# Two changes in one trunk kernel: softmax reciprocals spread by transfers, and the start of the up projection reordered

## The reference

```python
proj = (rmsnorm(x, norm1_g) * (1 + sc1) + sh1) @ w_in
y = concatenate([ssd_mixer(p_ssd), mla_mixer(p_mla), swa_sink_mixer(p_swa)]) @ w_out
x = x + g1 * y
h = rmsnorm(x, norm2_g) * (1 + sc2) + sh2
u = causal_dwconv(h @ ffn_w_up, ffn_conv_w, ffn_conv_b)      # width 3
a, b = split(u, 2)                                           # 2816 columns each
x = x + g2 * ((silu(a) * b) @ ffn_w_down)
```

## Time and profile before

| | |
|---|---|
| median of 3 runs | 2294.43 us (2293.14 to 2296.67) |
| the profiled execution's own time | 2295.75 us |
| its span | 2294.0 us |
| mean granted TensorE clock | 0.991 |
| attention, layer 0 | 326 to 431 us |
| start of the up projection, layer 0 | 541 to 606 us |

### The profile page before, as it was taken

One profiled execution on the slowest core, in us unless ns is written; L12 is line 12 of the kernel. 1 busy time (PEld: TensorE's weight loads), 2 busy tenths in 40 slices (PEclk: granted clock), 3 DMA queues, 4 the chain that ended last, 5 costly groups with the idle time before them and its releaser, 6 DMA issues.

```text
span 2294.0 us, 31143 instructions
## 1 busy us (share of the span) xinstructions
PE 2250.7 (98%) x11377; PEld 1844.6 (80%) x11377; DVE 1642.4 (72%) x2280; ACT 1104.0 (48%) x1818; POOL 974.6 (42%) x634
## 2 busy tenths in 40 slices
PE   6999999999999999999999999999999999999998
PEld 6887868887788888888878787788878888888887
DVE  7985466458878887778898744762796666667886
ACT  5355557444444444444543464772444444444455
POOL 3222322445988888300002124153399777760000
PEclk7999999999999999999999999999999999999999
DMA  9742220341444443577457222224323333337763
GB/s 331 283 136 69 66 74 20 129 143 43 160 127 140 118 142 106 170 280 252 146 211 249 63 70 62 50 86 132 105 83 97 115 93 117 94 124 272 255 203 115
DMA packets 273606, 317.13 MB, mean 138 GB/s; under 512 B 33869, under 2 KB 188288, under 8 KB 272687
## 3 DMA queue, kind: packets, MB, share of 16 engines
q1 hardware_dynamic: 271663, 312.11, 42.1%
q10 hardware_dynamic: 1072, 2.23, 0.4%
q0 software_dynamic: 720, 0.81, 0.1%
HBM read 248.37 MB, written 62.54 MB: 136 GB/s over the span
## 4 chain that ended last, share of the span: by engine, by line
PE 88%; POOL 4%; DVE 3%; issue 2%; DMA 1%; SPq 1%; ACT 1%; DVEq 0%; POOLq 0%; ACTq 0%
PE bank L1575 30%; PE bank L1135 19%; PE bank L1591 17%; PE bank L1192 7%; PE bank L1464 2%; PE bank L1429 1%; POOL prodLo L1760 1%; PE bank L1347 1%; PE bank L1394 1%; DVE hLo L2232 1%; POOL tLo L1764 1%; SPq L544 1%; PE bank L1396 1%; PE bank L1395 1%; PE bank L1387 1%
## 5 line engine op out<-in xcount | busy, mean ns | idle before, releaser
L1055 POOL TENSOR_TENSOR wLo<-raw,wHi 128x1024 fp32r<-128x1024 f32 x66 | 161.2, 2444 | 407.6 <-ACT wHi L1057 407.6
L1760 POOL TENSOR_TENSOR prodLo<-comb,prodHi 128x512 fp32r<-128x512 f32 x160 | 245.5, 1542 | 110.4 <-ACT prodHi L1097 110.4
L1575 PE MATMUL bank<-tHi,prodHi 128*128 128x512 f32 x640 | 251.2, 393 | 9.7 <-DVE part L2610 4.5
L1575 PE MATMUL bank<-tHi,prodLo 128*128 128x512 f32 x640 | 249.2, 389 | 0.0
L1575 PE MATMUL bank<-tLo,prodHi 128*128 128x512 f32 x640 | 249.1, 389 | 0.0
L1591 PE MATMUL bank<-gateHi,downHi 128*128 128x512 f32 x616 | 240.3, 390 | 0.1
L1591 PE MATMUL bank<-gateHi,downLo 128*128 128x512 f32 x616 | 239.7, 389 | 0.0
L1591 PE MATMUL bank<-gateLo,downHi 128*128 128x512 f32 x616 | 239.7, 389 | 0.0
L1097 ACT ACTIVATE prodHi<-comb 128x512 fp32r<-128x512 f32 x160 | 100.8, 632 | 260.5 <-PE bank L1575 242.7
L2588 DVE SCALAR_TENSOR_TENSOR ub<-bank,ffp,ub 128x1023 f32<-128x1023 f32 x88 | 112.8, 1282 | 103.3 <-ACT ub L2036 101.7
L1575 PE MATMUL bank<-hHi,prodLo 128*128 128x512 f32 x480 | 186.7, 389 | 0.0
(11 more groups left out here) (432 smaller groups left out, 5380.0 us busy)
## 6 DMA issues: line engine op xcount, KB each, us to landing
raw<-in_ffn_w_up_dram SPq DMA_DIRECT2D x88, 512.0 KB, 4.8
gateRaw<-gateOut SPq DMA_DIRECT2D x154, 256.0 KB, 4.2
adaE<-in_ada_w_dram SPq DMA_DIRECT2D x64, 512.0 KB, 6.4
gateOut<-gateSums SPq DMA_DIRECT2D x22, 1024.0 KB, 5.5
raw<-in_w_in_dram SPq DMA_DIRECT2D x34, 512.0 KB, 4.0
downRaw<-in_ffn_w_down_dram SPq DMA_DIRECT2D x66, 256.0 KB, 3.8
raw<-in_w_out_dram SPq DMA_DIRECT2D x28, 512.0 KB, 3.8
downCols<-in_ffn_w_down_dram SPq DMA_DIRECT2D x24, 512.0 KB, 3.6
```

The lines of the kernel that those rows point to most:

```text
L1055: eng.tensor_tensor(lo[:], raw[slot][:], fview(hi[:]), ALU.subtract).then_inc(s["split_lo"], 1)
L1575: last = mm(o, w[idx][:, c0], moving(idx, kp, hi), start=kp == 0 and q_ == 0, stop=kp == 3 and q_ == 2)
L1760: pool.tensor_tensor(sLoW[idx][:], product_source(js, idx), fview(sHiW[idx][:]), ALU.subtract).then_inc(s["us_lo"], 1)
```

## The change

Two changes together.

First, the reciprocals. `inverse_sums` and `copy_inverse` are gone. SyncE instead stores the four reciprocals of each of 128 queries as single values to HBM (`inv_out`, head by head), waits for it, and reads them back twice, each time spread over 64 partitions, into `invSum`. ScalarE copies the values' result from PSUM to `attOut` (`copy_block`, signal `sw_b`/`ml_b`), which frees the PSUM for the next block; VectorE multiplies `attOut` by `invSum` in place. `att_scaled` moves from one unit after the block's last to three, `att_hi` from two to four, `att_lo` from three to five; both tiles have four buffers instead of two. All but the last block's transfers stand in SyncE's order ahead of the load of the output projection's third pack, with the row sums' among them; the last block's stand between the two loads of x. In the output projection steps 4 and 5 of both packs move behind all others.

Second, the up projection's start. VectorE splits six tiles of tLo (4, 5, 6, 7, 0, 1) instead of four, GpSimd two instead of four. GpSimd makes all four combinations of js = 0 before the low part of its third product. At js = 0 VectorE does `taps(1, 1)`, `result(0, 0)`, `result(0, 1)`, `taps(1, 0)`, and both gates after `result(0, 2)`; at js = 1 the gate comes after `result(1, 2)`. ScalarE's `first_product(0)` comes after the six remainders and its own high parts.

```diff
+            def spread_inverse(n):
+                kind, i = DONE[n]
+                sp.wait_ge(s["sw_r" if kind == "s" else "ml_r"], nth("sw_r" if kind == "s" else "ml_r", i + 1))
+                sp.dma_start(inv_out[n].rearrange("h q -> q h"), stat[kind][:, i % 3, 2, :], allow_slow_non_contiguous=True).then_inc(s["iv_stored"], 16)
+                sp.wait_ge(s["iv_stored"], nth("iv_stored", 16 * (n + 1)))
+                if n >= 4:
+                    banded, latent = settled(n)
+                    sp.wait_ge(s["sw_x"], nth("sw_x", banded))
+                    sp.wait_ge(s["ml_x"], nth("ml_x", latent))
+                for a in range(2):
+                    sp.dma_start(bcs[n % 4][64 * a:64 * a + 64, :].rearrange("p (j q) -> p j q", j=2),
+                                 inv_out[n:n + 1].rearrange("o (j a) q -> a o j q", a=2)[a].to_broadcast([64, 2, P])).then_inc(s["sw_c" if kind == "s" else "ml_c"], 16)
...
                 if n == N_OUT0 + 2:
-                    store_rstd()
-                    spread_rstd()
+                    ended = [u for u in range(NU) if LAST[UNITS[u][0]][UNITS[u][1]] == u]
+                    for d, u in enumerate(ended[:-1]):
+                        if u > TURN_AT and ended[d - 1] <= TURN_AT:
+                            store_rstd()
+                            spread_rstd()
+                        spread_inverse(d)
                 if n == N_OUT0 + 3:
 
                     sp.wait_ge(s["un_o"], nth("un_o", PV_BY[LAST["s"][NB - 1]]))
                     sp.dma_start(xT[:, 0:4, :], xtail[:, 0:4, :]).then_inc(s["tail_loaded0"], 16)
+                    spread_inverse(len(DONE) - 1)
...
-                    kind, i, _ = UNITS[u - 1]
-                    if LAST[kind][i] == u - 1:
-                        inverse_sums(kind, i)
...
-            out_steps(0, (3, 6, 7, 4, 5))
-            out_steps(1, (0, 1, 2, 3, 6, 7, 4, 5))
+            out_steps(0, (3, 6, 7))
+            out_steps(1, (0, 1, 2, 3, 6, 7))
+            out_steps(0, (4, 5))
+            out_steps(1, (4, 5))
...
-                    pe.wait_ge(s["t_lo_pool"], nth("t_lo_pool", 4))
+                    pe.wait_ge(s["t_lo_pool"], nth("t_lo_pool", 2))
+                    pe.wait_ge(s["t_lo_dve"], nth("t_lo_dve", 6))
...
-                if js == 0:
-                    product_lo(0, 2)
...
-            for kp in range(4):
+            for kp in range(2, 4):
                 t_lo(kp)
...
-            def copy_inverse(kind, i):
-                act.wait_ge(s["sw_b" if kind == "s" else "ml_b"], nth("sw_b" if kind == "s" else "ml_b", i + 1))
+            def copy_block(kind, i):
+                act.wait_ge(s["un_o"], nth("un_o", PV_BY[LAST[kind][i]]))
...
-                    for w, todo in ((u - 1, copy_inverse), (u - 2, att_hi)):
+                    for w, todo in ((u - 1, copy_block), (u - 4, att_hi)):
...
-                first_product(js)
                 if js == 0:
                     act.wait_ge(s["t_lo_dve"], nth("t_lo_dve", 4))
                     for idx in range(4, PRODUCTS):
                         product_hi(act, 0, idx)
+                    act.wait_ge(s["t_lo_dve"], nth("t_lo_dve", 6))
+                first_product(js)
...
-                dve.tensor_tensor(ytk[n % 2][:], half(3, 0 if kind == "s" else 1)[:, 0:256], bcs[n % 2][:], ALU.mult).then_inc(s["sw_x" if kind == "s" else "ml_x"], 1)
+                dve.wait_ge(s["sw_c" if kind == "s" else "ml_c"], nth("sw_c" if kind == "s" else "ml_c", 32 * (i + 1)))
+                dve.wait_ge(s["sw_b" if kind == "s" else "ml_b"], nth("sw_b" if kind == "s" else "ml_b", i + 1))
+                dve.tensor_tensor(ytk[n % 4][:], ytk[n % 4][:], bcs[n % 4][:], ALU.mult).then_inc(s["sw_x" if kind == "s" else "ml_x"], 1)
...
-                for w, todo in ((u, inverse_of), (u - 1, att_scaled), (u - 3, att_lo)):
+                for w, todo in ((u, inverse_of), (u - 3, att_scaled), (u - 5, att_lo)):
...
+            for k in (4, 5, 6, 7, 0, 1):
+                dve.wait_ge(s["t_hi"], nth("t_hi", 2 * (k - 4) + 2 if k >= 4 else 2 * k + 1))
+                dve.tensor_tensor(tLo[:, k, :], xT[:, k, :], fview(tHi[:, k, :]), ALU.subtract).then_inc(s["t_lo_dve"], 1)
...
+                if js == 0:
+                    taps(1, 1)
+                    result(0, 0)
+                    result(0, 1)
+                    taps(1, 0)
+                else:
+                    taps(j - 1, 1)
+                    taps(j - 1, 0)
+                    result(js, 0)
+                if js > 1:
                     gate(j - 1)
+                for i in range(1 if js else 2, 6):
                     result(js, i)
+                    if js == 0 and i == 2:
                         gate(0)
                         gate(1)
+                    if js == 1 and i == 2:
+                        gate(j - 1)
```

More of the change, by code:

```diff
@@ L189, with settled @@
 N_PV = sum(PAIR_END)
+def settled(n):
+    return N_INV_S[n - 3], n - 3 - N_INV_S[n - 3]
 PER_LAYER = {
@@ L318, in build @@
     stat = {k: place(f"stat_{k}", [P, 3, 3, 4], F32, R[13] + 8320 + 192 * n) for n, k in enumerate("sm")}
-    bcs = [place(f"invSum{i}", [P, 256], F32, R[11] + K * i) for i in range(2)]
-    ytk = [place(f"attOut{i}", [P, 256], F32, R[11] + 2 * K + K * i) for i in range(2)]
+    bcs = [place(f"invSum{i}", [P, 256], F32, at["f"] + K * i) for i in range(4)]
+    ytk = [place(f"attOut{i}", [P, 256], F32, R[11] + K * i) for i in range(4)]
     spreadA = place("cumSpread", [P, 8, P], F32, E[0])
@@ L1465, in values @@
                 last.then_inc(s["un_o"], 1)
[L1467 to L1473, removed]
             y_hi = [yHi[:, j, :] for j in range(4)] + [mHi[:, j, :] for j in range(2)] + [sHi[:, j, :] for j in range(2)]
@@ L1778, in _ @@
                 combos(js)
-                for idx in range((3, 2)[js] if js < 2 else 0, PRODUCTS):
+                for idx in range(2 if js < 2 else 0, PRODUCTS):
                     product_lo(js, idx)
@@ L1977, in att_hi @@
                 dst = sHi if kind == "s" else mHi
-                A(dst[:, :, i * BLK:(i + 1) * BLK], ytk[N_INV[kind][i] % 2][:].rearrange("p (k t) -> p k t", k=2), ACT.Copy).then_inc(s["sw_hi" if kind == "s" else "ml_hi"], 1)
+                A(dst[:, :, i * BLK:(i + 1) * BLK], ytk[N_INV[kind][i] % 4][:].rearrange("p (k t) -> p k t", k=2), ACT.Copy).then_inc(s["sw_hi" if kind == "s" else "ml_hi"], 1)
             exps(0)
-            for u in range(NU + 2):
+            for u in range(NU + 4):
                 def finish():
@@ L2088, in _ @@
             base(1)
-            act.wait_ge(s["t_lo_pool"], nth("t_lo_pool", 4))
             for js in range(FT - N_STD):
@@ L2517, in _ @@
             least(1)
-            for u in range(NU + 3):
+            for u in range(NU + 5):
                 if u + 2 < NU:
@@ L2658, in _ @@
             taps(0, 1)
-            for kp in range(4):
-                dve.wait_ge(s["t_hi"], nth("t_hi", 2 * kp + 2))
-                dve.tensor_tensor(tLo[:, 4 + kp, :], xT[:, 4 + kp, :], fview(tHi[:, 4 + kp, :]), ALU.subtract).then_inc(s["t_lo_dve"], 1)
+            for k in (4, 5, 6, 7, 0, 1):
+                dve.wait_ge(s["t_hi"], nth("t_hi", 2 * (k - 4) + 2 if k >= 4 else 2 * k + 1))
+                dve.tensor_tensor(tLo[:, k, :], xT[:, k, :], fview(tHi[:, k, :]), ALU.subtract).then_inc(s["t_lo_dve"], 1)
             for js in range(FT - N_STD):
@@ L2668, in _ @@
                     next_product(2 * (js - NEXT_JS) + 1)
-                taps(j - 1, 1)
-                taps(j - 1, 0)
-                result(js, 0)
-                if js:
+                if js == 0:
[8 more added lines that the diff above has]
+                if js > 1:
                     gate(j - 1)
-                for i in range(1, 6):
+                for i in range(1 if js else 2, 6):
                     result(js, i)
-                    if js == 0 and i == 1:
+                    if js == 0 and i == 2:
                         gate(0)
-                    if js == 0 and i == 2:
                         gate(1)
+                    if js == 1 and i == 2:
+                        gate(j - 1)
                     if js == 0 and i >= 2:
```

31 lines of the change are left out of this document (13 added, 18 removed).

## The result

The changed kernel takes 2493.48 us, median of four runs (2490.25 to 2495.98), where the kernel before took 2295.23 (2293.14 to 2296.67). The ratio is 1.0865, with a 95% interval of 1.0850 to 1.0881. I had forecast 2289.2 in a range of 2280 to 2298, so the prediction was wrong by 204 us. What happened is rival E, to which I had given 0.08, and some eight times dearer than the 2320 at which I had priced it (198 us over before, not 25).

The account below looks back on a forecast made before the run. TensorE, busy 98%, was taken to bound the kernel. From 2295.75 us, - 14.1 - 5.5 + 1.0 + 0.4 + 9.6 + 3.4 = - 5.2 gave 2290.5; the runs' median being 1.3 lower, 2289.2, range 2280 to 2298.

Parts of the forecast that it names:

- rival E: Attention: store of single values landing at 6 us holds SyncE 7.4 us a block against 6.3; 2320 us, chance 0.08.
- the detour: Attention, reciprocal to scaling: store, its landing, two spreads and their landing take 5.4 us (4 to 7), hidden.
- The threshold: Attention: up to 8.3 us from reciprocal to scaling nothing happens; over it VectorE stands at each scaling, PE behind.
- The matmuls taken out: Attention: 32 groups spreading the reciprocals leave PE, 0.44 us each, saving 14.1 us.
- VectorE's scaling beside GpSimd: Attention: scalings from SBUF slow down during GpSimd's work; 0.5 us a layer reaches PE, 1.0 in sum.
- The junction: After attention's last block: PE waits 4.8 us a layer before the second output pack, 9.6 in sum.
- the early need alone: Second output pack: PE needs its low part earlier; without any transfer in the way the wait is 1.0 us.
- rival C: The wait after attention's last block eats all the gain: 8 us a layer with clock falls, 2296 us, chance 0.17.
- The clock: Behind PE's wait for the second output pack: one fall to 1.2 GHz a layer, 1.7 us each, 3.4 in sum.
- Part two: Start of the up projection: reordered remainders, combinations and gates shrink PE's gaps, giving 5.5 us (2 to 8).
- My first gap: Start of the up projection: PE's first gap becomes 0.9 us instead of 1.93.
- the give-back at the third tile: Up projection, layer 0: GpSimd's first low part of that tile ends at 603.5, PE asks at 602.1; 1.4 us lost.

Follow-up runs that it names:

- b16_by_query: Changed kernel with the 2 KB store written query by query, 128 pieces of 16 bytes instead of 512 of 4, read-back unchanged (scales wrong): 2295.2 us, ratio 0.9995.
- s16_apart: Changed kernel with the 512 single values of 4 bytes each written 16 bytes from the next: 2302.0 us.
- b32_pieces: Changed kernel storing 512 pieces of 32 bytes instead of 512 of 4 (scales mixed up): 2302.7 us, ratio 1.0032.
- s32_apart: Changed kernel with the 512 single values of 4 bytes each written 32 bytes from the next: 2304.8 us.
- s8_aligned: Changed kernel with single values written 8 bytes apart, eight to 64 bytes, each 64 bytes from one run of eight queries: 2328.4 us.
- s8_moved: Changed kernel with single values 8 bytes apart and the tensor moved by 32 bytes, so each 64 bytes holds values of two runs of queries: 2336.0 us.
- s64_apart: Changed kernel with the 512 single values of 4 bytes each written 64 bytes from the next (scales wrong): 2326.4 us.
- ceiling_none: Changed kernel without storing and spreading reciprocals, invSum filled once with 1.0 (division left out): 2278.11 us, ratio 0.9941.
- experiment 5: Changed kernel with 16-byte pieces and a right result; then SyncE's order at the junction changed, then ScalarE's too: 2302.12, 2294.25 and 2283.14 us.
- p2_up_only: Kernel before with the up projection's edits alone, attention as before: 2288.06 us, ratio 0.9968.
- experiment 1: Each part alone: kernel before with only the up projection's edits, 2288.06 us; changed kernel without them, 2490.29 us.
- part_two_alone: Second run of the kernel before with the up projection's edits alone: 2287.78 us, ratio 0.9972.
- the three mended kernels: Changed kernel with 16-byte pieces and a right result: by itself, with SyncE's order changed, and with ScalarE's order changed too: 2302.12, 2294.25 and 2283.14 us.
- p1_att_only: Changed kernel without the up projection's edits, attention part alone: 2490.29 us, ratio 1.0849.
- fix_layout: Changed kernel with 16-byte pieces, spreads of 511 floats, VectorE reading with a 16-byte step, three invSum tiles, result right: 2302.12 us, ratio 1.0035.
- fix_layout_junction: fix_layout with the last block's transfers ahead of the load of x and ScalarE's second-pack split ahead of the last high part: 2283.14 us, ratio 0.9958.

## Why the prediction was wrong

The step that failed is one term of the detour, the landing of the store of reciprocals: "From below stands the one of the row sums (8 KB, 1.4 us to landing), from above the small weight pieces (32 KB, 3.0); I take 2.3". It was 9.8. Both bounds had been chosen by bytes. Neither row has single values in it, so neither was an upper bound, and the trace of before held none. The sentence on the 512 descriptors stood in the prediction, but only as a rule without a price; it should have widened the bounds. Yet the count that this rule gives isn't the price either: 128 pieces side by side cost as much, and 512 apart a third.

What came of each step:
- **The threshold** of 8.3 us fits the runs. By the prediction's own sum (0.8 and the two landings) the detour is 14.4 us in the changed kernel (store 9.8, spread 3.8 where I had 2.3), and VectorE stood idle 227.0 us, at 29 of 32 scalings. With median detours of 5.4 (b16_by_query), 6.5, 6.8 and 7.0 (s16_apart, b32_pieces, s32_apart) it stood 9.9, 12.7, 17.2 and 22.1 us; with 7.8, 8.0 and 8.7 (s8_aligned, s8_moved, s64_apart, whose spreads landed in 4.0) 61.9, 70.8 and 53.4.
- **Rival E** had the mechanism to the letter, SyncE held longer than the blocks are apart. Its own formula with the measured landing gives 9.8 + 1.4 = 11.2 us a block against 6.3, 16 x 4.9 = 78 us a layer; measured 89.0 and 85.2. With 6 us it had given 18. What was wrong is its chance and the landing at which it was priced (its own 18 us a layer, on top of 2289.2, also make 2325 and not 2320).
- **The matmuls taken out** (14.1): with nothing else in the way, 9.9 of them arrived, as 14.1 less the junction's need (2.2) and VectorE's part (1.6) says to within 0.4.
- **VectorE's scaling beside GpSimd** (1.0): 1.6 in ceiling_none, and 2.5 of waits for probT in b16_by_query. Small, as forecast.
- **The junction** (4.8 a layer): with the landing near my 2.3, in b16_by_query, it was 5.0 and 4.9 us, and both of its causes are real (experiment 5). That the early need alone makes 1.0 is borne out by ceiling_none (1.1 in each layer). In the changed kernel the store of the last block (issued 515.65, 0.6 us behind the 2 MB of x) held SyncE until 529.60, and TensorE's wait was 16.0 us, twice the 8 of rival C.
- **The clock** (1.7 a layer): it fell, and for longer. From 439.8 to 450 us, behind the wait of b16_by_query, TensorE was busy 10.14 us at a mean granted clock of 0.74, so about half of the stretch at 1.2 GHz, and 10.20 x 0.26 = 2.6 us of work were lost:

```profile
439.80:450.00 10.20, 10.14 (x34) 8.22 (x35) 0.00 (x0) 0.00 (x0) 2.33 (x2) 0.74 0.41 127
```

  In the changed kernel it was also low inside attention, where TensorE now stands idle for up to 12.4 us at a time; 340 to 360 us, where before had 20.00 busy and 0.91:

```profile
340.00:360.00 20.00, 11.04 (x66) 9.30 (x67) 5.10 (x19) 5.47 (x17) 0.00 (x0) 0.66 0.11 13
```

- **Part two** (2.25 in layer 0, 3.25 in layer 1): the sum of 5.5 became 7.3 by the ratio, and 6.4 by that of the same kernel's second run. In the output projection of layer 1 the matmuls below begin at 1564.2 instead of 1568.0, of which 0.9 was there before the first up projection, so layer 0 gave 2.9 and layer 1 the last 4.4 of the span's 8.2. The 0.9 isn't part two's: the clock from 340 to 360 us was 1.00 in p2_up_only's profiled execution, 0.91 in that of before. My first gap of 0.9 is one of 0.73 as the profile counts it (0.89 with the 0.16 of the modelled end), the second closed, and the third is gone, where I had left 0.85. (The prediction's gains in layer 0, 1.9 and 2.58 - 0.85, also make 3.6, not 3.8.)

```profile
L1192 PE MATMUL bank<-ssdHi,wHi x48: 389/389/486, 1568.0 to 1631.3; 128*128 128x512 f32 x48
```

```profile
L1192 PE MATMUL bank<-ssdHi,wHi x48: 388/390/486, 1564.2 to 1627.5; 128*128 128x512 f32 x48
```

  In layer 0 the give-back at the third tile, forecast at 1.4, is the wait of 1.0 for prodLo shown in experiment 1.

With a store near what I took, b16_by_query came to 2295.2, inside my range but still 6 over my 2289.2. Its profiled execution was the slowest of its ten (2299.4), and shows a term that no step of mine had: the clock inside attention, with TensorE busy throughout. From 340 to 360 us it was 0.74, some 3.4 us below the 0.91 of the kernel before, and from 1455 to 1475 us 0.91, another 1.8; the last values of layer 0 started at 430.3, against 430.5 before. This isn't of the change alone, as p2_up_only and part_two_alone, one and the same kernel, differ by it too (shown in the last section). How much of the 6 us in the median is of this kind is open, since only one execution has a trace.

## What to carry to other kernels

Price a small store by the form of its pieces, not by its bytes, and when no row of the trace has that form, say that there is no upper bound and measure it first. Values of a partition that leave side by side as one piece (here four reciprocals in 16 bytes, read back with a step) landed in 1.8 to 2.4 us (median of b16_by_query and of the three mended kernels) where the transposing store took 9.8, and that alone was worth nearly 8% of the kernel. A transfer that stands in a queue's order between two waits sets the pace by its landing, not by its issue: compare what holds the queue with the distance of the blocks, and put the late small store ahead of the big load that isn't urgent.

## What the runs showed of the hardware

- Single values of 4 bytes written side by side to HBM were through the queues 1.5 us after the issue, in the store shown, and landed 7 us later; 128 take as long as 512 (9.9 and 9.8 us). At 8 bytes apart they take 4.3, at 16 and 32 about 3, at 64 again 3.9, each from one execution. The same 2 KB in pieces of 16 bytes take 1.8. I had expected only the number of pieces to count.
- The same transposing store had a median landing of 9.3 us in p1_att_only and 9.8 in the kernel after, and the first attention, alike in both, differed by 7 us.
- VectorE's 128x256 multiplication of two SBUF tiles took 0.39 to 0.42 us while GpSimd rested (b16_by_query, ceiling_none) and 0.59 to 0.62 (fix_layout, fix_layout_junction) where one input is read with a step of 16 bytes; beside GpSimd's work single ones took up to 1.32 without the step and 1.35 with it.
- The granted clock in one stretch of attention differs between executions of one kernel, without a gap in TensorE's work. From 340 to 360 us, p2_up_only, part_two_alone (the same kernel) and b16_by_query:

```profile
340.00:360.00 20.00, 20.00 (x192) 16.88 (x193) 12.62 (x43) 14.00 (x42) 0.00 (x0) 1.00 0.01 2
```

```profile
340.00:360.00 20.00, 20.00 (x182) 16.76 (x181) 11.48 (x37) 12.94 (x38) 0.00 (x0) 0.91 0.00 1
```

```profile
340.00:360.00 20.00, 20.00 (x134) 16.71 (x134) 9.60 (x34) 10.60 (x35) 0.00 (x0) 0.74 0.12 26
```

  The clock of an execution goes with its time: three of ceiling_none's four had a mean of 0.993 and took 2277.6 to 2278.2 us, one had 0.988 and took 2288.4, a step larger than all of part two. What decides it, no run shows.
